# Two-by-two blocks with seven products in the MLP down projections of a two-layer encoder

## The reference

```python
def squared_relu_mlp(x, w1, w2):
    return jnp.square(jax.nn.relu(x @ w1)) @ w2
...
        h = layer_norm(DN_ALPHA * h + y, ln_g[i, 0], ln_b[i, 0])   # y: attention or gated linear attention
        f = squared_relu_mlp(h, mlp_w1[i], mlp_w2[i])
        h = layer_norm(DN_ALPHA * h + f, ln_g[i, 1], ln_b[i, 1])
```

## Time and profile before

| | us |
|---|---|
| three runs, median (lowest to highest) | 2218.16 (2215.19 to 2218.85) |
| the profiled execution | 2218.2 |
| its span | 2216.5 |
| TensorE busy | 2200.0 |
| TensorE's weight loads | 1882.2 |
| VectorE busy | 1261.6 |
| ScalarE busy | 898.0 |
| GpSimd busy | 108.8 |
| read from HBM | 414.00 MB, 188 GB/s over the span |

### The profile page before, as it was taken

One profiled execution on the slowest core, in us unless ns is written; L12 is line 12 of the kernel. 1 busy time (PEld: TensorE's weight loads), 2 busy tenths in 40 slices (PEclk: granted clock), 3 DMA queues, 4 the chain that ended last, 5 costly groups with the idle time before them and its releaser, 6 DMA issues.

```text
span 2216.5 us, 28804 instructions
## 1 busy us (share of the span) xinstructions
PE 2200.0 (99%) x11324; PEld 1882.2 (85%) x11324; DVE 1261.6 (57%) x1074; ACT 898.0 (41%) x757; POOL 108.8 (5%) x94
## 2 busy tenths in 40 slices
PE   8999999999999999999999999999999999999998
PEld 7888888988888888888888888889888888888886
DVE  5554555854554555455676566658555645554655
ACT  4443442443343443343454344334434434433431
POOL 3000000200000000000020111102000000000000
PEclk9999999999999999999999999999999999999999
DMA  8545545654655555655446445647555546655542
GB/s 297 170 161 178 186 179 205 226 190 165 217 188 190 194 188 174 214 190 176 162 144 220 165 151 184 233 152 247 172 210 192 185 170 214 197 194 190 186 163 107
DMA packets 206640, 417.04 MB, mean 188 GB/s; under 512 B 6688, under 2 KB 6688, under 8 KB 205552
## 3 DMA queue, kind: packets, MB, share of 16 engines
q1 hardware_dynamic: 204528, 405.82, 53.9%
q0 software_dynamic: 1472, 9.25, 1.1%
q10 hardware_dynamic: 576, 1.05, 0.2%
HBM read 414.00 MB, written 2.10 MB: 188 GB/s over the span
## 4 chain that ended last, share of the span: by engine, by line
PE 99%; issue 0%; DVE 0%; DMA 0%; POOLq 0%; POOL 0%; ACT 0%; SPq 0%
PE ps L438 97%; PE ps L509 1%; DMA res<-in_x_dram 0%; PE ps L755 0%; PE ps L603 0%; DVE res L1252 0%; PE ps L584 0%; DVE res L1243 0%; DVE X L1071 0%; POOLq L89 0%; POOL ln_rstd L346 0%; DVE ln_stats L1205 0%; DVE res L1079 0%; ACT X L815 0%; SPq L293 0%
## 5 line engine op out<-in xcount | busy, mean ns | idle before, releaser
L1059 DVE TENSOR_TENSOR lo<-raw,hi 128x2048 fp32r<-128x2048 f32 x384 | 881.8, 2302 | 570.8 <-ACT hi L790 569.4
L790 ACT ACTIVATE hi<-raw 128x2048 fp32r<-128x2048 f32 x383 | 732.7, 1917 | 917.5 <-PE ps L438 904.1
L438 PE MATMUL ps<-hi,F 128*128 128x512 f32 x2560 | 793.2, 390 | 0.0
L438 PE MATMUL ps<-X,hi 128*128 128x512 f32 (+1 forms) x3008 | 704.0, 379 | 1.6 <-DVE X L1071 1.6
L438 PEld LDWEIGHTS ps<-X,hi 128*128 128x128 f32 x3008 | 545.3, 190 | 96.4 <-DVE X L1071 1.8
L438 PEld LDWEIGHTS ps<-hi,F 128*128 128x128 f32 x2560 | 480.6, 188 | 99.6
L438 PE MATMUL ps<-lo,F 128*128 128x512 f32 x1280 | 498.1, 389 | 0.0
L438 PE MATMUL ps<-X,lo 128*128 128x256 f32 x2816 | 388.5, 283 | 0.0
L438 PEld LDWEIGHTS ps<-X,lo 128*128 128x128 f32 x2816 | 374.6, 192 | 12.8
L438 PEld LDWEIGHTS ps<-lo,F 128*128 128x128 f32 x1280 | 240.4, 188 | 49.1
L438 PE MATMUL ps<-hi,X 128*128 128x512 f32 x768 | 246.7, 396 | 0.0
(11 more groups left out here) (114 smaller groups left out, 534.0 us busy)
## 6 DMA issues: line engine op xcount, KB each, us to landing
raw<-in_mlp_w_dram SPq DMA_DIRECT2D x256, 1024.0 KB, 5.2
raw<-in_gla_w_in_dram SPq DMA_DIRECT2D x48, 1024.0 KB, 5.2
raw<-in_attn_w_qkv_dram SPq DMA_DIRECT2D x47, 1024.0 KB, 5.2
raw<-in_attn_w_o_dram SPq DMA_DIRECT2D x16, 1024.0 KB, 5.7
raw<-in_gla_w_o_dram SPq DMA_DIRECT2D x16, 1024.0 KB, 5.3
work<-in_ln_g_dram POOLq DMA_DIRECT2D x4, 1024.0 KB, 7.3
work<-in_ln_b_dram POOLq DMA_DIRECT2D x4, 1024.0 KB, 9.9
res<-in_x_dram SPq DMA_DIRECT2D x8, 256.0 KB, 8.4
```

The lines of the kernel that those rows point to most:

```text
L438: return pe.matmul(o, w, m, start=start, stop=stop)
L790: act.activation(hi[:, j], raw[:, j], ACT.Copy).then_inc(hi_ready, 1)
L1059: dve.tensor_tensor(lo[:, j], raw[:, j], hi[:, j].bitcast(F32), ALU.subtract).then_inc(lo_ready, 1)
```

## The change

In each chunk, the first two down groups (columns 0 to 1023) and the first half of the depth (tiles 0 and 1) are treated as a product of two-by-two blocks: two row blocks of 128 by two depth halves of 512 times two depth halves by two column groups. Seven block products take the place of eight. Their operands are partly sums: four sums of weight tiles (`w_sum`, made in place in `raw`), and four sums of row blocks of the activations (`forms`, with hi and lo parts, S1 to S4). Each of the seven weight operands gets its own hi and lo split (`quarter_hi`, `quarter_lo`), before it was four tiles. Products 0, 2, 4 and 6 go into bank 0 one on top of the other, and DVE adds or subtracts the bank's content to parts of `res` between them (`add_part`); TensorE waits for that (`res_added`). Products 1 and 5 share bank 1, product 3 has bank 3. The second half of the depth of both column groups follows as before, tile by tile, in banks 3, 0, 1 and 2. Groups three and four are as before. The fourth up group's activations are now finished beside and behind the products. Group numbers count nine slots of four tiles a chunk (`STEP`). The forms lie in the front of `work`, so POOL's load of the MLP's normalisation gain and bias waits until the products of the last chunk are used. SP's chunk loop is unrolled, the other engines' chunk loops run over the two middle chunks, with the first and last written out.

```diff
                     sp.dma_start(raw[:, j], w[:, bass.ds(row + KPT * j, KPT), bass.ds(col, COLS)]
                                  ).then_inc(raw_full[j], 16)
+            def load_quarters(g, w, row):
+                for j, (k, n) in enumerate(((0, 0), (0, 1), (1, 1), (1, 0))):
+                    sp.wait_ge(lo_ready, 4 * g + j - 3)
+                    sp.dma_start(raw[:, j], w[:, bass.ds(row + KPT * k, KPT), n * COLS:(n + 1) * COLS]
+                                 ).then_inc(raw_full[j], 16)
+            def load_rest(g, w, row):
+                for j, (n, k) in enumerate(((0, 2), (0, 3), (1, 2), (1, 3))):
+                    sp.wait_ge(lo_ready, 4 * g - (3, 3, 2, 0)[j])
+                    sp.dma_start(raw[:, j], w[:, bass.ds(row + KPT * k, KPT), n * COLS:(n + 1) * COLS]
+                                 ).then_inc(raw_full[j], 16)
             for q in range(QUARTERS):
                 c = slice(q * COLS, (q + 1) * COLS)
                 for t in range(TB):
@@ -303,11 +326,13 @@
                 load_group(q + G_WO, w_o, COLS * q)
             def load_mlp(m):
-                with sp.Fori(0, CHUNKS) as ch:
+                for ch in range(CHUNKS):
                     with sp.Fori(0, QUARTERS) as q:
-                        load_group(8 * ch + q + G_MLP[m], w_1[m], D * ch + COLS * q)
-                    with sp.Fori(0, QUARTERS) as q:
-                        load_group(8 * ch + q + (G_MLP[m] + 4), w_2[m], COLS * q, KT * ch)
+                        load_group(STEP * ch + q + G_MLP[m], w_1[m], D * ch + COLS * q)
+                    load_quarters(STEP * ch + (G_MLP[m] + 4), w_2[m], KT * ch)
+                    load_rest(STEP * ch + (G_MLP[m] + 6), w_2[m], KT * ch)
+                    with sp.Fori(2, QUARTERS) as q:
+                        load_group(STEP * ch + q + (G_MLP[m] + 5), w_2[m], COLS * q, KT * ch)
             load_mlp(0)
...
-            pool.wait_ge(ln_quarter, 8)
+            pool.wait_ge(w_used, 4 * (G_MLP[0] + STEP * (CHUNKS - 1) + 6))
...
-            def down_first(m, ch, g, n, r):
-                rows_late(g, F, lambda j: (f_lo, 8 * ch + (32 * m + 2 * j + 2)),
-                          ((halves_added, 2 * n - 2), (halves_added, 2 * n)))
+            def product(g, p, bank, stationary, start, stop):
+                def mm(o, w, m, first, last):
+                    return pe.matmul(o, w, m, start=first, stop=last or not start, skip_group_check=not start)
+                acc = ps[:, bank, :]
+                pe.wait_ge(hi_ready, 4 * g + p + 1)
+                for k in range(KPT):
+                    a_hi, a_lo = stationary(k)
+                    mm(acc, a_hi, hi[:, p % TILES, k, :], start and k == 0, False)
+                    mm(acc, a_lo, hi[:, p % TILES, k, :], False, False)
+                pe.wait_ge(lo_ready, 4 * g + p + 1)
+                for k in range(KPT):
+                    a_hi, a_lo = stationary(k)
+                    m = mm(acc, a_hi, lo[:, p % TILES, k, :], False, stop and k == KPT - 1)
+                m.then_inc(w_used, 2 if p == PRODUCTS - 1 else 1)
+            def first_pair(m, ch, g, n, r):
+                def plain(k0, t):
+                    return lambda k: (F[:, k0 + k, 0, blk(t)], F[:, k0 + k, 1, blk(t)])
+                def form(f):
+                    return lambda k: (forms[:, f, k, 0, :], forms[:, f, k, 1, :])
+                u = 4 * ch + 4 * CHUNKS * m
+                pe.wait_ge(halves_added, 2 * n - 2)
+                pe.wait_ge(f_lo, 8 * ch + (32 * m + 4))
+                product(g, 0, 0, plain(0, 0), True, True)
+                pe.wait_ge(form_lo, u + 4)
+                product(g, 1, 1, form(S1), True, True)
+                pe.wait_ge(res_added, 2 * r + 1)
+                product(g, 2, 0, form(S2), False, True)
+                product(g, 3, 3, plain(KPT, 0), True, True)
+                pe.wait_ge(res_added, 2 * r + 3)
+                product(g, 4, 0, form(S3), False, True)
+                pe.wait_ge(res_added, 2 * r + 2)
+                product(g, 5, 1, form(S4), False, True)
+                pe.wait_ge(res_added, 2 * r + 4)
+                product(g, 6, 0, plain(KPT, 1), False, True)
+                for p, (c, j) in enumerate(((0, 2), (0, 3), (1, 2), (1, 3))):
+                    pe.wait_ge(lo_ready, 4 * g + 8 + p + 1)
+                    pe.wait_ge(f_lo, 8 * ch + (32 * m + 2 * j + 2))
+                    for t in range(TB):
+                        acc = ps[:, ((3, 0), (1, 2))[c][t], :]
+                        for k in range(KPT):
+                            a = 4 * j + k
+                            first = c == 1 and t == 1 and p == 2 and k == 0
+                            pe.matmul(acc, F[:, a, 0, blk(t)], hi[:, p, k, :], start=first, stop=True,
+                                      skip_group_check=not first)
+                            pe.matmul(acc, F[:, a, 0, blk(t)], lo[:, p, k, :], start=False, stop=True,
+                                      skip_group_check=True)
+                            e = pe.matmul(acc, F[:, a, 1, blk(t)], hi[:, p, k, :], start=False, stop=True,
+                                          skip_group_check=True)
+                    e.then_inc(w_used, 1)
+            def third_group(g, n, r):
+                pe.wait_ge(res_added, 2 * r - 2)
+                rows_pass(g, 0, F)
+                pe.wait_ge(halves_added, 2 * n)
+                rows_pass(g, 1, F)
             def mlp(m, L):
                 g0, n0, r0 = G_MLP[m], COLS_MLP[m], RES_MLP[m]
                 up_pair(m, L, g0, n0, r0, True)
                 up_pair(m, L, g0 + 2, n0 + 2, r0, False)
-                down_first(m, 0, g0 + 4, n0 + 4, r0)
-                out_groups(g0 + 5, r0 + 1, 3, F)
+                first_pair(m, 0, g0 + 4, n0 + 4, r0)
+                third_group(g0 + 7, n0 + 4, r0 + 4)
+                out_groups(g0 + 8, r0 + 5, 1, F)
                 with pe.Fori(1, CHUNKS - 1) as ch:
+                    g, n, r = STEP * ch + g0, 4 * ch + n0, 6 * ch + r0
                     with pe.Fori(0, 2) as p:
-                        up_pair(m, L, 8 * ch + 2 * p + g0, 4 * ch + 2 * p + n0, 4 * ch + r0, False)
-                    down_first(m, ch, 8 * ch + (g0 + 4), 4 * ch + (n0 + 4), 4 * ch + r0)
-                    with pe.Fori(0, 3) as q:
-                        pe.wait_ge(res_added, 8 * ch + 2 * q + (2 * r0 + 1))
...
-            def up_window(g, n, par, k, fk):
-
-                split_some(g + 1, 3)
-                copy_halves(g, n, par, mlp_half)
-                split_hi(g + 1, 3)
+            def quarter_hi(g, p, j, f, u):
+                if p in (0, 3, 5):
+                    act.wait_ge(raw_full[j], 16 * f + 16)
+                else:
+                    act.wait_ge(w_summed, u + {1: 1, 2: 3, 4: 2, 6: 4}[p])
+                act.wait_ge(w_used, 4 * g + p - 3)
+                act.activation(hi[:, p % TILES], raw[:, j], ACT.Copy
+                               ).then_inc(hi_ready, 2 if p == PRODUCTS - 1 else 1)
+            def form_hi_of(f, at, count):
+                act.wait_ge(form_summed, count)
...
+                for s in range(2):
+                    act.activation(hidden[e][:, 2 * s:2 * s + 2, :], ps[:, 4 * e + 2 * s:4 * e + 2 * s + 2, SEQ:],
+                                   ACT.Copy).then_inc(half_copied, 1)
+            def f_hi_of(e, k, fk):
                 for s in range(2):
                     act.wait_ge(squared, k + (s + 1))
-                    act.activation(F[:, bass.ds(fk + 2 * s, 2), 0, :], mlp_hidden[:, s], ACT.Copy).then_inc(f_hi, 1)
+                    act.activation(F[:, fk + 2 * s:fk + 2 * s + 2, 0, :], hidden[e][:, 2 * s:2 * s + 2, :],
+                                   ACT.Copy).then_inc(f_hi, 1)
+            def chunk(m, ch, g, f, n, first, last):
+                k = 8 * ch + 32 * m
+                u = 4 * ch + 4 * CHUNKS * m
+                for e in range(3):
+                    split_some(g + e + 1, 3, f + (e + 1))
+                    down_halves(g + e, n + e, e % 2, k + 2 * e, u + 3 if e == 2 else None, first and e < 2)
+                    split_hi(g + e + 1, 3, f + (e + 1))
+                    f_hi_of(e % 2, k + 2 * e, 4 * e)
+                    if e == 0:
+                        form_hi_of(S3, 0, u + 1)
+                    elif e == 1:
+                        form_hi_of(S1, 1, u + 2)
+                        form_hi_of(S2, 0, u + 3)
+                        form_hi_of(S4, 1, u + 4)
+                quarter_hi(g + 4, 0, 0, f + 4, u)
+                quarter_hi(g + 4, 1, 0, f + 4, u)
+                quarter_hi(g + 4, 2, 0, f + 4, u)
+                quarter_hi(g + 4, 3, 3, f + 4, u)
+                quarter_hi(g + 4, 4, 1, f + 4, u)
+                quarter_hi(g + 4, 5, 2, f + 4, u)
+                quarter_hi(g + 4, 6, 3, f + 4, u)
+                down_halves(g + 3, n + 3, 1, k + 6, u + 4, False)
+                split_some(g + 6, 2, f + 5)
+                f_hi_of(1, k + 6, 12)
+                split_hi(g + 6, 2, f + 5)
```

(118 more changed lines are left out.)

149 lines of the change are left out of this document (73 added, 76 removed).

## The result

The changed kernel took **2198.01 us** in the median of 4 runs (2197.34 to 2198.61), the kernel before 2216.68 us (2214.98 to 2218.85, 4 runs) beside it: ratio 0.9916 [0.9904, 0.9928], a gain of 18.7 us where 16.6 were forecast. The profiled execution took 2197.34 us, with a span of 2195.6 us.

A forecast was written before the change was run, and what follows sets the result against it. The prediction took TensorE's matmul rate to bound the kernel: 2218.2 us, less 21.8 for 96 matmuls left out, plus 5.2 for idle behind the products, made 2201.6 us, with a range of 2195 to 2214.

The forecast's parts named there:

- What bounds the kernel: Whole span: TensorE's matmul rate sets the time; each matmul left out saves 0.2267 us, 96 of them 21.8 us.
- The rival at 0.13 us each: Removed matmuls free less than 0.2267 us each, so the gain is 12.6 us and the time 2210; chance 4%.
- The feeders' cost lies beside other work: Per chunk, 24 us more on VectorE and 8 us on ScalarE, with no term of its own in the sum.
- The schedule of the seven products: First two down groups of each chunk: seven products run within some 0.05 us of their own pace, 19.04 us.
- The four gates: Points where TensorE's products need operands or a bank ready; all said to be met by 0.0 to 0.4 us.
- The longer chain: Rival: 12 links to the rest's first tile, 0.1 us more each, idle 1.85 us a chunk, 2211; chance 19%.
- The idle behind the products: TensorE waits after product 6 for the rest's first tile: 0.65 us a chunk, 5.2 us over 8 chunks.
- the middle between landings of 5.2 and 5.9 us: Raw slot 0's reload: idle 0.3 us at 5.2, 1.0 at 5.9; the forecast took 0.65 us.
- The first of the pair: Load into raw slot 0, issued 0.4 us before slot 1's; expected to land undisturbed in 5.2 us at best.
- the near end: The 5.2 us median landing of raw slot 0's reload, which would leave TensorE 0.3 us idle a chunk.
- The slower rival: Raw slot 0's reload lands late, up to 10.5 us: 5.6 us idle a chunk, 45 in all, 2241 us; chance 9%.
- The base of the sum: The starting time of the forecast: 2218.2 us, the profiled execution of the kernel before, taken without correction.

The follow-up runs named there:

- e3: The changed kernel with the four weight sums left out, so four products take single weight tiles: 2194.43 us, ratio 0.99.
- e2: The changed kernel with one more 128x2048 VectorE instruction a chunk, between the residual update after product 0 and the fourth weight sum: 2227.12 us, ratio 1.0047.
- e7: The changed kernel with two small 128x512 VectorE instructions a chunk, between the residual update after product 0 and the fourth weight sum: 2212.13 us.
- e6: The changed kernel with the loads of the rest's first two tiles issued one split later, after product 5's lo and not product 4's: 2240.03 us.

## Why the prediction was right

- **What bounds the kernel**: right. TensorE's matmul count sets the time, and e3 gives 2.72 us for twelve, the price worked out from 22 triples. The rival at 0.13 us each is out.
- **The feeders' cost lies beside other work**: right. VectorE's 24 us and ScalarE's 8 us a chunk show up in their busy times, and in the span only as the 0.28 us below. VectorE got 179 us and not 194: queued operations overlap by some 0.1 us (4.49 for two of 2.29), and the forecast multiplied durations. It entered no term of the sum.
- **The schedule of the seven products**: right, each step within 0.2 us. The four gates were met to 0.1 us. The longer chain, 0.1 us more at each link, is out; that there is no slack is shown by e2 and e7.
- **The idle behind the products**: right in place and sign, its size off. The term was 0.65 us a chunk, 5.2 in all; measured 0.28, 2.2 in all. The failed choice is the middle between landings of 5.2 and 5.9 us. The first of the pair landed in 5.0 to 5.2 us in all eight chunks (in the one above ScalarE starts on it 5.18 behind the issue) and the second in 7.3 to 7.4: they followed one another, so the near end was the whole answer. The Trainium skill, DMA: Bandwidth & Descriptors, section Queues, rings and completion order, has the descriptors of one ring consumed in order; these pairs agree. With the load that early, VectorE's own queue sets the moment as much as the load.
- **The slower rival**: its mechanism was right (e6), its condition wasn't given. Its price was too low, since it had no lower clock behind the idle time.
- **The base of the sum and the start**: what the prediction didn't see. The execution from which it starts held 3.1 us of lowered clock in the mixer; the earlier trace rows give the clock in tenths and averaged over 55 us, and a fall of some 6 us looks like 9 there. A run without it is 3 us faster with no change at all. The start, 1.7 us longer, had no term. From the forecast to the profiled execution after are 2201.6 - 2197.3 = 4.3 us: some 3.0 from the idle term and 3.1 from the base one way, 1.7 from the start the other. That the last two nearly cancel is luck. Gain against gain it looks closer, 16.6 against 18.7, because the median before, 2216.68, lies 1.5 us under the base of the sum and mixes runs with more and less of the fall. By the down parts alone the change is worth 19.5 us.

## What to carry to other kernels

Where the busiest engine never waits, an instruction taken from it is worth its start-to-start distance, provided that the feeders' orders are laid side by side with real durations up to the moment at which the chain rejoins; the gain hangs on that one place. Two loads issued together on one queue were not two that share: in all eight pairs here the first was as fast as alone (5.0 to 5.2 us, 5.2 in the median before). And compare kernels by the stretch that the change touches: whole times held 1.5 to 3 us that came from the clock elsewhere, and 0.4 to 2.3 us from the start.

## What the runs showed that was not expected

- **A gap can lower the clock behind it.** From matmul to matmul, 1.5 to 1.6 us (e7) left the granted clock at 1.00 in all eight chunks; 2.4 to 2.5 us (e2) had 0.50 behind it in six and cost some 1.4 us more each, but of the four gaps of 2.40 us two had it and two didn't; 3.4 to 3.65 us (e6) had it in all eight, some 1.5 to 2.8 us. Waits on a TensorE-bound path can cost more than their length; e6's 2240 is made up that way.
- **A clock fall without a gap.** In the second mixer the clock fell to 0.51 behind matmuls with 16-row stationary tiles, with TensorE busy throughout, in some executions and not in others of the same kernel: 0, 1.5 or 3.1 us. What decides it stays open.
- **The sum of two f32 tiles costs what a split costs** on VectorE: 2285 against 2289 ns at 128x2048.
